# The first attention's compressed branch: one float32r product of 96 rows in place of an fp32 product

## The reference

```
hdn = silu(einsum("bnlhd,ldf->bnhf", kb, w1))      # kb: overlapping blocks of 32 tokens, 15 of them
vc  = einsum("bnhf,fe->bnhe", hdn, w2)             # compressed values: 15 per key head, width 128
...
p_c = where(cvalid, softmax(where(cvalid, q . kc * scale, NEG)), 0)
o_c = einsum("bhgqn,bnhe->bqhge", p_c, vc)         # per query head: [256 x 15] times [15 x 128]
out = gate0 * o_c + gate1 * o_s + gate2 * o_w      # o_s, o_w: selected and window branch
```

## Time and profile before

| | us |
|---|---|
| runs | 2268.53, 2270.15, 2270.98 |
| median | 2270.15 |
| the profiled execution | 2270.24 |
| its span | 2268.6 |
| TensorE busy | 2255.1 (99%) |
| DVE busy | 1554.2 (69%) |
| ACT busy | 1106.3 (49%) |

### The profile page before, as it was taken

One profiled execution on the slowest core, in us unless ns is written; L12 is line 12 of the kernel. 1 busy time (PEld: TensorE's weight loads), 2 busy tenths in 40 slices (PEclk: granted clock), 3 DMA queues, 4 the chain that ended last, 5 costly groups with the idle time before them and its releaser, 6 DMA issues.

```text
span 2268.6 us, 31288 instructions
## 1 busy us (share of the span) xinstructions
PE 2255.1 (99%) x10413; PEld 1867.9 (82%) x10413; DVE 1554.2 (69%) x1938; ACT 1106.3 (49%) x1439; POOL 148.7 (7%) x283
## 2 busy tenths in 40 slices
PE   9999999999999999999999999999999999999998
PEld 8888888888888888888888888888888888888886
DVE  6676777777775555888777776666655666665566
ACT  6455445566664444533366554445444443444444
POOL 1000110000000000011011210000000000000000
PEclk9999999999999999999999999999999999999999
DMA  8788896555565766697588887666666666666554
GB/s 307 271 286 287 313 338 242 204 208 198 205 234 173 282 221 213 205 334 272 195 292 306 302 301 250 242 202 219 218 211 218 229 225 230 224 217 207 204 208 145
DMA packets 150602, 546.52 MB, mean 241 GB/s; under 512 B 17265, under 2 KB 18032, under 8 KB 148992
## 3 DMA queue, kind: packets, MB, share of 16 engines
q1 hardware_dynamic: 112416, 405.92, 51.3%
q0 software_dynamic: 34688, 129.64, 16.7%
q10 hardware_dynamic: 3424, 9.96, 1.1%
HBM read 534.92 MB, written 10.53 MB: 240 GB/s over the span
## 4 chain that ended last, share of the span: by engine, by line
PE 94%; DVE 3%; DMA 2%; ACT 1%; issue 0%; POOL 0%; DVEq 0%; SPq 0%; ACTq 0%
PE ps L1862 23%; PE ps L1864 23%; PE ps L1863 23%; PE ps L1981 6%; PE ps L1983 5%; PE ps L1982 5%; PE ps L1901 3%; PE ps L2087 1%; DMA ada<-wa_dram 1%; PE ps L2036 1%; DVE w_lo L1094 1%; DMA raw<-ws_dram 1%; PE ps L1877 1%; PE ps L1879 1%; PE ps L1878 1%
## 5 line engine op out<-in xcount | busy, mean ns | idle before, releaser
L1094 DVE TENSOR_TENSOR w_lo<-raw,w_hi 128x1024 fp32r<-128x1024 f32 x758 | 923.6, 1224 | 596.0 <-ACT w_hi L630 580.7
L630 ACT ACTIVATE w_hi<-raw 128x1024 fp32r<-128x1024 f32 x750 | 792.5, 1061 | 999.1 <-PE ps L1864 847.2
L1862 PE MATMUL ps<-w_hi,a_hi 128*128 128x512 f32 x1612 | 629.9, 391 | 0.0
L1864 PE MATMUL ps<-w_hi,a_lo 128*128 128x512 f32 x1612 | 627.5, 389 | 0.0
L1863 PE MATMUL ps<-w_lo,a_hi 128*128 128x512 f32 x1612 | 627.3, 389 | 0.0
L1864 PEld LDWEIGHTS ps<-w_hi,a_lo 128*128 128x128 f32 x1612 | 302.6, 188 | 63.3
L1862 PEld LDWEIGHTS ps<-w_hi,a_hi 128*128 128x128 f32 x1612 | 302.7, 188 | 62.1 <-DVE a_lo L1312 0.3
L1863 PEld LDWEIGHTS ps<-w_lo,a_hi 128*128 128x128 f32 x1612 | 302.7, 188 | 61.7
L1981 PE MATMUL ps<-w_hi,a_hi 128*128 128x512 f32 x640 | 258.6, 404 | 0.6 <-DVE w_lo L1094 0.6
L1983 PE MATMUL ps<-w_hi,a_lo 128*128 128x512 f32 x640 | 249.9, 390 | 0.0
L1982 PE MATMUL ps<-w_lo,a_hi 128*128 128x512 f32 x640 | 249.4, 390 | 0.0
(11 more groups left out here) (322 smaller groups left out, 2180.1 us busy)
## 6 DMA issues: line engine op xcount, KB each, us to landing
raw<-ws_dram SPq DMA_DIRECT2D x768, 512.0 KB, 4.2
ada<-wa_dram POOLq DMA_DIRECT2D x192, 512.0 KB, 5.0
gates_spill<-gst ACTq DMA_DIRECT2D x16, 512.0 KB, 6.0
ga<-gates_spill POOLq DMA_DIRECT2D x8, 512.0 KB, 4.3
gb<-gates_spill POOLq DMA_DIRECT2D x8, 512.0 KB, 5.6
bias_c<-b_merge_dram POOLq DMA_DIRECT2D x9, 256.0 KB, 4.9
cb<-c_dram POOLq DMA_DIRECT2D x2, 1024.0 KB, 6.3
x<-x_dram POOLq DMA_DIRECT2D x2, 1024.0 KB, 8.5
```

The source lines that it names most:

```text
L630: act.activation(w_hi[:, k.slot(RING), :], raw[:, k.slot(RING), :], ACT.Copy).then_inc(hi_done, 1)
L1094: dve.tensor_tensor(w_lo[:, k.slot(RING), :], raw[:, k.slot(RING), :], w_hi[:, k.slot(RING), :].bitcast(F32), ALU.subtract).then_inc(lo_do ...
L1862: pe.matmul(o, hi(m, tb), w_hi[:, s, cols], start=m == 0, stop=False)
L1864: mm = pe.matmul(o, lo(m, tb), w_hi[:, s, cols], start=False, stop=m == of * kts - 1)
```

## The change

The compressed product becomes one float32r product. The split is laid along the contraction: the weights `vcg` hold, for one key head, the rounded values in rows 0-14, the rest of the values in rows 32-46, and the rounded values again in rows 64-78. The transposed probabilities hold the rounded probabilities in rows 0-14 and again in 32-46, and the rest of them in rows 64-78. Their sum over the rows is hi*hi + lo*hi + hi*lo. The unrounded probabilities stand in rows 80-94, against zeros.

- DVE, per unit: the gate-over-sum multiply now writes to column 80 on, and is waited for; a copy rounds it to columns 0 and 32; after the scaling of `prob`, a subtraction writes the rest to column 64 on, before `p_ready`.
- For `vc`: the hidden values are copied three times by ACT into `hdnV`, which has 96 columns per key head and is zeroed by DVE first, so that the products with `w2` give three copies of the values in one piece (96 rows). ACT rounds all rows, then DVE replaces rows 32-63 by the difference.
- `vcg` and `pcT` get the type float32r; TensorE's product keeps its place.

```diff
-        pcT = at("pcT", SC + 20 * K, [PC_W, 2 * P])
+        pcT = at("pcT", SC + 20 * K, [PC_W, 2 * P], F32R)
-        vcg = at("vcg", SC + 26 * K, [PC_W, HD])
+        vcg = at("vcg", SC + 26 * K, [PC_W, HD], F32R)
-        vc = at("vc", R + 6 * K, [N_CMP, NKV, HD])
+        vc = at("vc", R + 6 * K, [PC_V, NKV, HD], F32R)
+        hdnV = at("hdnV", SC + 2 * K, [P, 2, NKV, PC_V])
...
-                    act.activation(vcg[0:N_CMP], vc[:, i, :], ACT.Copy).then_inc(a.v_ready, 1)
+                    act.activation(vcg[0:PC_V], vc[:, i, :].bitcast(F32), ACT.Copy).then_inc(a.v_ready, 1)
...
+                    act.wait_ge(hdnV_zero, 1)
+                    for r in range(0, PC_V, 32):
+                        e = act.activation(hdnV[:, :, :, r:r + N_CMP],
+                                           ps[:, 4, 0:2 * CMP_ROWS].rearrange("p (f h n) -> p f h n", f=2, h=NKV), ACT.Copy)
...
-            act.activation(vc[:], ps[0:N_CMP, 5, :], ACT.Copy).then_inc(cmp_ready, 1)
+            act.activation(vc[:], ps[0:PC_V, 5, :].rearrange("p (h d) -> p h d", h=NKV), ACT.Copy).then_inc(vc_hi, 1)
...
-                            chain.on(dve.tensor_tensor(pcj, pcj, cden[:].unsqueeze(2).to_broadcast([P, 2, N_CMP]),
-                                                       ALU.mult))
+                            pcp = pc[:, j % 2, :, PC_P:PC_P + N_CMP]
+                            link(dve.tensor_tensor(pcp, pcj, cden[:].unsqueeze(2).to_broadcast([P, 2, N_CMP]),
+                                                   ALU.mult))
+                            pch = pc[:, j % 2, :, 0:64].bitcast(F32R).rearrange("p h (r n) -> p h r n", r=2)[:, :, :, 0:N_CMP]
+                            chain.on(dve.tensor_copy(pch, pcp.unsqueeze(2).to_broadcast([P, 2, 2, N_CMP])))
+                            rounded = chain.n
...
                         chain.on(dve.tensor_tensor(pj, pj, cf[:].unsqueeze(2).to_broadcast([P, 4, w]), ALU.mult))
+                        if nsa_:
+                            dve.wait_ge(dve_chain, rounded)
+                            chain.on(dve.tensor_tensor(pc[:, j % 2, :, 64:64 + N_CMP], pcp, pcj, ALU.subtract))
                         dve.wait_ge(dve_chain, chain.n)
                         dve.sem_inc(a.p_ready, 1)
...
+            dve.memset(hdnV[:], 0.0).then_inc(hdnV_zero, 1)
...
+            dve.wait_ge(vc_hi, 1)
+            dve.tensor_tensor(vc[32:64], ps[32:64, 5, :].rearrange("p (h d) -> p h d", h=NKV), vc[32:64].bitcast(F32),
+                              ALU.subtract).then_inc(cmp_ready, 1)
...
-                        mm = pe.matmul(ps[0:N_CMP, 6 - n, h * HD:(h + 1) * HD],
-                                       hdnT[:, n, f, h * N_CMP:(h + 1) * N_CMP], w2[:, n, f, :],
+                        rows, hidden = ((N_CMP, hdnT[:, f, h * N_CMP:(h + 1) * N_CMP]), (PC_V, hdnV[:, f, h, :]))[n]
+                        mm = pe.matmul(ps[0:rows, 6 - n, h * HD:(h + 1) * HD], hidden, w2[:, n, f, :],
                                        start=f == 0, stop=f == 1)
```

More of the change, by code:

```diff
@@ L53 @@
 CMP_H = 2 * HD
-PC_W = 100
+PC_W, PC_V, PC_P = 100, 96, 80
 GRID_W, NA_ROWS, NA_COLS = 64, 8, 16
@@ L273, in build @@
         hdn = at("hdn", SC + 24 * K, [CMP_ROWS, CMP_H])
-        hdnT = at("hdnT", SC + 25 * K, [P, 2, 2, CMP_ROWS])
+        hdnT = at("hdnT", SC + 25 * K, [P, 2, CMP_ROWS])
         prob = at("prob", SC, [P, 2, 4, S])
@@ L327, in build @@
         ck_ready, kb_sum, kb_hi_done, kb_ready = sem("ck_ready"), sem("kb_sum"), sem("kb_hi_done"), sem("kb_ready")
+        vc_hi, hdnV_zero = sem("vc_hi"), sem("hdnV_zero")
         hdn_ready, hdnT_done, hdnT_ready, w2_in = sem("hdn_ready"), sem("hdnT_done"), sem("hdnT_ready"), sem("w2_in")
@@ L411, in build @@
         CMP_COL = NC - 2 * HD // 8
-        CH_NSA = 80
+        CH_NSA = 88
         def score(k, w):
@@ L885, in hidden_turned @@
                 act.wait_ge(hdnT_done, n + 1)
-                act.activation(hdnT[:, n, :, :], ps[:, 4, 0:2 * CMP_ROWS], ACT.Copy).then_inc(hdnT_ready, 1)
+                if n == 0:
+                    act.activation(hdnT[:], ps[:, 4, 0:2 * CMP_ROWS].rearrange("p (f r) -> p f r", f=2), ACT.Copy)\
+                        .then_inc(hdnT_ready, 1)
+                else:
+                    act.wait_ge(hdnV_zero, 1)
+                    for r in range(0, PC_V, 32):
+                        e = act.activation(hdnV[:, :, :, r:r + N_CMP],
+                                           ps[:, 4, 0:2 * CMP_ROWS].rearrange("p (f h n) -> p f h n", f=2, h=NKV), ACT.Copy)
+                    e.then_inc(hdnT_ready, 1)
             evict(0, At(G0["kcvc"]), ACT.Copy)
@@ L1300, in _ @@
             dve.sem_inc(gate_used, 1)
-            link(dve.memset(vcg[:], 0.0))
+            link(dve.memset(vcg[:].bitcast(F32), 0.0))
             dve.memset(squares[:, 1, 0:P], 0.0).then_inc(zeros_in, 1)
```

## The result

| | before | after |
|---|---|---|
| median | 2270.3 us (2268.53 to 2270.98) | 2291.55 us (2287.88 to 2292.13) |
| ratio | | 1.0093 (95% interval 1.0081 to 1.0105) |
| span of the profiled execution | 2268.6 us | 2289.5 us |
| mean granted clock of TensorE | 0.999 | 0.994 |

The account below looks back on a forecast made before the run. TensorE's stream was taken as the bound (busy 84.98 of 85.00 us). 5.1 us saved less 4.5 us given back as waits on VectorE's longer chain gave -0.6 us: 2269.6 us, range 2266.8 to 2272.4.

Parts of the forecast that it names:

- what is added per unit on DVE: Each unit's DVE chain gains a wait, a copy of 60 elements and a subtraction of 30, together 0.36 us.
- d: Time added to each unit's DVE chain ahead of p_ready: 0.36 us, bounds 0.30 and 0.55.
- The slower rival: DVE's added wait, copy and subtraction cost 0.8 us a unit through queue instructions: +4.7 us, 2274.9; chance 0.05.
- the saving on TensorE: Compressed product in one float32r pass, 0.12 us instead of 0.44, 16 times: 5.1 us saved.
- The rival in which float32r isn't cheap: TensorE's product with 128 weight columns takes 0.22 us, saving only 0.22: 2270.0 us; no separate chance given.
- The rival without any overlap: DVE instructions don't overlap around the new ones, d = 0.55: +1.7 us, 2271.9; chance 0.09.
- where d ends up: Unit 0's d is lost in a gap, units 1 to 3 add 3d; TensorE waits 1.14 us a group before unit 3.
- the place differs, the sum does not: Part of TensorE's wait may fall at 423.01 (0.96 us), the rest at unit 3; only unit 3's p_ready counts.
- the forecast's own sum: Four groups, each 3d less 0.90 us of cover less 0.32 saved by the fourth product: -0.6 us.
- no wait at all: Rival: an unseen gap takes up DVE's delays, TensorE keeps all 5.1 us: 2265.1 us; chance 0.06.
- the one-time additions: Memset 0.75 us and subtraction on DVE, copies up to 0.54 us on ACT, all in idle stretches: nothing booked.

Follow-up runs that it names:

- e15: The changed kernel whole, with 8 unused semaphore increments of VectorE ahead of its loop over the groups, so that it begins at 321: 2270.07 us in one run.
- e5: The changed kernel whole, with 16 unused semaphore increments of VectorE ahead of its loop of 264 instructions: 2269.59 us, ratio 0.9998.
- e1: The changed kernel with VectorE's chain of the kernel before, without the rounding copy and the subtraction of the probabilities; float32r product kept: 2266.11 us, ratio 0.9978.
- e14: The kernel before with 16 unused VectorE increments in its loop (264 instructions) and 272 ahead of it: 2299.2 us in one run.

## Why the prediction was wrong

- **Failed: the account of what is added per unit on DVE.** It priced the added instructions by their time (d) alone. The count of instructions stood in no term, yet it is what decided: 264 from instruction 313 on touch three blocks of 256 by the reading above, while the same 264 eight instructions later cost nothing (e15). The price is 7.3 us at each of three returns, 22 us, four times the saving that was hoped for.
- **The slower rival had the right sign and the wrong mechanism.** It wanted d above 0.79 us from added waits with their queue instructions. d is 0.33. With the fetches known as a mechanism but not the place of the border, the forecast should have been two cases, near 2270 and near 2290.
- **Right: the saving on TensorE.** One record, 0.12 us instead of 0.44; products of units 0 and 1 start 11.95 us apart (404.01, 415.96) instead of 12.27. The rival in which float32r isn't cheap falls.
- **Right: d**, 0.36 forecast, 0.33 measured. The copy follows the rule of the other small ones (0.11) and didn't need the extra 0.03. The rival without any overlap, 0.55, falls by the same rows. It leaned on the first half of a paragraph: the section "The DRAIN you can't avoid" of the Trainium skill's page "VectorE: DVE Perf Modes" goes on to say that a next instruction which is not held starts earlier, so these rows don't speak against it as a whole.
- **Half right: where d ends up.** The chain of delays is there, and so is the wait. But "the place differs, the sum does not" doesn't hold at the d that was measured: the wait lies at unit 2's transposes (423), with 2d and 0.34 us of cover where I had guessed 0.4, and little of it is left for unit 3. A group wins 0.32 us instead of 0.14, 4 x 0.32 = 1.3 in all instead of 0.6. (With d = 0.33 the forecast's own sum gives 4 x (0.99 - 1.22) = -0.9, so about half of the gap is the size of d.) e5 came out at 2269.59, 0.6 below the kernel before that was measured beside it. That it meets the forecast of 2269.6 is luck: 1.3 won, less some 0.7 that its increments cost TensorE in the first group. Its interval (-2.5 to +1.6 us) holds both sums.
- **Right: no wait at all would be worth more.** The rival gave 2265.1. With d = 0 (e1) it was 2266.1, since 0.30 us a group is lost even then.
- **Not seen apart:** the one-time additions (memset, copies, the subtraction out of PSUM). The first product starts at 404.01 instead of 403.92; other executions of this stage differ by more.

## What to carry to other kernels

Before a loop body grows, count the instructions that it has as compiled on each engine, waits' register additions included, and see where it begins. By the reading above, up to 256 touch two blocks wherever they lie (every run with 248 to 256 was free of the stall), above that it depends on the place, and a few idle instructions ahead of the loop can move it, at a price of their own (TensorE waited 0.28 us for 8 and 0.7 us for 16 here). In a profile the mark is idle time "<- issue" on the first instruction of the body, at each return, together with several packets on the instruction queue at that time (five a return here; a single one stands in e14 and e15 too, which lose nothing by it). And where an engine has several anchors on a late chain, work out the wait at each of them, since the first to bind sets the sum.

## What the runs showed of the hardware

- A loop of 264 instructions on VectorE that begins at instruction 312, 313 or 568 idles it 6.9 to 8.0 us at every return (20.8 and 23.9 us for three, with 15 packets on the instruction queue), where 0.7 is usual; beginning at 321, 329 or 584 it has none of this. A loop of 312 beginning at 328 has none either.
- After 4.86 us without work TensorE's matmuls of 512 columns start 0.43 us apart instead of 0.23 (1.2 instead of 2.4 GHz), and the first twelve take 5.1 us. In this kernel that made a stall half as long again: 2.4 us on 4.86.
- A semaphore increment that nobody waits for takes about 0.1 us on VectorE (24.87 us of idle time for 256). 16 in one place cost VectorE 1.6 us where it is needed, and 16 ahead of the loop cost TensorE 0.7 us.
